# Hymba and PEER layer: the second norm by token half, two projection groups and six query groups re-split, and a last stage of four blocks by token half

## The chip, the cores and the metric
The kernel runs on one core of one Trainium2 chip. Its engines are TensorE (PE in the profile, its weight loads PEld), VectorE (DVE), ScalarE (ACT), GpSimd (POOL) and SyncE (SP), which here only issues the loads. Each runs its own list of instructions in order and waits for the others at semaphores. The metric is the time of one execution on the device in microseconds.

## What is computed
One layer on a sequence of 256 tokens and 1024 channels, float32. The reference, cut to the parts that the change touches:

```python
mod = silu(c) @ w_ada + b_ada
sh1, sc1, g1, sh2, sc2, g2 = split(mod, 6)
h = rmsnorm(x, norm1_g) * (1 + sc1) + sh1
proj = h @ w_in                      # q, k, v of 4 differential heads and 8 block heads
mix = concat(diff_attention, block_attention) @ w_out
x = x + g1 * mix
h2 = rmsnorm(x, norm2_g) * (1 + sc2) + sh2
q = h2 @ peer_wq                     # 8 heads x 2 keys of 128
s1, s2 = q[:, :, 0] . keys1, q[:, :, 1] . keys2     # 128 scores a list, 16 lists
# top 16 of each list, top 16 of their 256 sums: 16 experts a head
x = x + g2 * sum(softmax(score) * gelu(h2 . u[expert]) * v[expert])
out = rmsnorm(x, final_g)
```

## The kernel before
Tokens are two halves of 128 (index t), channels eight chunks of 128 (index c). A number is split where full precision is wanted with fast products: a rounded copy (high, made by ScalarE) and what is left (low, a subtraction on VectorE or GpSimd); a product of two such numbers is three products, high by high, low by high, high by low. A product of unsplit float32 is one instruction of the program and two records of the trace.

Weights come in groups of 256 columns (GROUPS): 0 to 11 for w_in, 12 to 15 for w_out (WO), 16 to 23 for the queries (WQ).

Start: the row c is loaded to all 128 partitions (crow) and put through Silu by ScalarE. VectorE forms the columns of sh1 and sc1 as sums over crow, two per chunk (L1104), ScalarE normalises x together with VectorE (nat), TensorE turns it to columns (L688), ScalarE scales it (hT). Each chunk then meets the weights of groups 0 to 5 (whole_chunk), the first chunks plain (L764, L768), later ones split (L795 to L805).

Attention: 16 units a (8 differential, 8 block ones). For each TensorE makes the scores (L850), VectorE adds the bias (logits, L1216), ScalarE takes the exponential (exps), VectorE weighs the two maps of a differential unit (combine), TensorE transposes (L869) and weighs v (L885). Between the units TensorE works off the projection groups 6 to 11 in quarters (STEPS, proj_step), four a unit, all plain. Into the gaps of VectorE the function sums(a, n) puts the columns of sc2 (units 3 to 6), the row of g1 (7 to 10) and the first columns of sh2. After unit LATE + 1 it multiplies the differential heads by their norm.

Then come the four groups of the output projection (out_highs, out_lows), the residual by group (residual), the sums of squares, the second norm of both token halves at once and the transposes (L688). The eight query groups follow (query_high, query_lows, query_group), with the high copies by ScalarE (high_group) and the low parts by VectorE for group 0 and by GpSimd for 1 to 7 (L430); beside them VectorE adds up the row of g2 (gate_sum, L1091 and L1094). Then 32 score products (L966).

The longest part streams 256 blocks of expert weights, 128 of u and 128 of v: a load into one of five slots, high (L605), low (GpSimd L439 or VectorE L1367), products. While blocks 0 to 46 of u run, VectorE sorts; blocks in SORT_LOW have their low part made by VectorE in the middle of the sort, the others below POOL_LOW = 46 by GpSimd, all later ones by VectorE. The last LAST blocks of v are done by token half, so that the last norm of half 0 runs beside half 1.

SyncE issues all loads in program order, on one queue, with the waits that free their places.

## Time and profile before
| | us |
|---|---|
| median of 3 runs | 980.34 (980.28 to 980.77) |
| the profiled execution | 980.4 |
| its span, first to last instruction | 978.5 |
| TensorE busy in it | 947.8 (97%) |
| VectorE, ScalarE, GpSimd busy | 718.8, 468.2, 161.8 |
| first product of the projection | 15.16 |
| first product of the output projection | 127.6 |
| first score product | 209.1 |
| first product with v blocks | about 622 |

Times in the rows are microseconds from the start of the span. A row of a timeline gives start, duration, engine, line, what is written and read, how many, and in brackets how long the engine was idle before it and what released it. "issue" is time for which the profile shows no wait. The line numbers are those of the kernel before.

### The profile page before, as it was taken

The numbers are of one execution on the slowest core, as the hardware profiler recorded it, in microseconds if no ns is written. First come the engines' busy times: TensorE is split into PE (matmuls) and PEld (weight loads), VectorE is DVE, ScalarE is ACT, GpSimd is POOL, SyncE is SP. The second block draws the span as 40 slices with busy tenths as digits, with TensorE's granted clock in tenths as the row PEclk, the third lists the DMA queues.
The fourth block names the chain that finished last, engine by engine and source line by source line (L and its number), as shares of the span: only waits on it lengthen the run. The fifth ranks groups of instructions, "written<-read, shape, count | busy, mean of one in ns | idle before, by whom it ended". The sixth has DMA issues, their size and how long they took to land.

```text
span 978.5 us, 16499 instructions
## 1 busy us (share of the span) xinstructions
PE 947.8 (97%) x6426; PEld 864.5 (88%) x6426; DVE 718.8 (73%) x1388; ACT 468.2 (48%) x856; POOL 161.8 (17%) x83
## 2 busy tenths in 40 slices
PE   4999998999999999999999999999999999999996
PEld 3987798999999999999999999888888888888885
DVE  4738888729999888999999995655555555555556
ACT  3443665444444534444444444455555555555554
POOL 1000003959889810000000000000000000000000
PEclk9999998999999999999999999999999999999999
DMA  8999457026665555554455555666666666666663
GB/s 341 357 399 436 194 238 317 28 109 184 184 182 185 179 166 159 161 157 152 152 156 166 153 152 176 185 195 191 194 193 195 192 196 191 193 195 194 192 194 115
DMA packets 47900, 193.14 MB, mean 197 GB/s; under 512 B 5312, under 2 KB 7504, under 8 KB 46544
## 3 DMA queue, kind: packets, MB, share of 16 engines
q1 hardware_dynamic: 47760, 192.07, 59.6%
q8 instruction: 51, 0.84, 0.4%
q14 instruction: 25, 0.20, 0.1%
q0 software_dynamic: 64, 0.03, 0.0%
HBM read 191.00 MB, written 1.07 MB: 196 GB/s over the span
## 4 chain that ended last, share of the span: by engine, by line
PE 89%; DVE 4%; POOL 3%; ACT 1%; DMA 1%; issue 1%; SPq 0%; DVEq 0%; ACTq 0%
PE banks L1010 23%; PE banks L986 12%; PE banks L990 12%; PE banks L1017 12%; PE banks L987 12%; PE banks L768 4%; PE banks L1001 3%; POOL wq_low L430 3%; PE banks L764 2%; PE banks L734 2%; PE banks L700 1%; PE banks L802 1%; DMA small_cols<-in_cols 1%; PE banks L751 1%; PE banks L885 1%
## 5 line engine op out<-in xcount | busy, mean ns | idle before, releaser
L1367 DVE TENSOR_TENSOR lo<-raw,hi 128x1024 fp32r<-128x1024 f32 x214 | 267.6, 1251 | 170.5 <-ACT hi L605 169.2
L605 ACT ACTIVATE hi<-raw 128x1024 fp32r<-128x1024 f32 x256 | 271.5, 1061 | 169.7 <-PE banks L1017 169.7
L986 PE MATMUL banks<-h2r,hi 128*128 128x256 f32 x1024 | 256.4, 288 | 0.0
L987 PE MATMUL banks<-h2r,hi 128*128 128x256 f32 x1024 | 251.1, 283 | 0.0
L1010 PE MATMUL banks<-hi,wsplit 128*128 128x512 f32 x1000 | 247.0, 389 | 0.5 <-DVE wsplit L1460 0.5
L1010 PEld LDWEIGHTS banks<-hi,wsplit 128*128 128x128 f32 x1000 | 187.6, 188 | 39.6 <-issue 0.7
L987 PEld LDWEIGHTS banks<-h2r,hi 128*128 128x128 f32 x1024 | 196.5, 192 | 0.0
L986 PEld LDWEIGHTS banks<-h2r,hi 128*128 128x128 f32 x1024 | 196.0, 191 | 0.0
L990 PE MATMUL banks<-h2r,lo 128*128 128x256 f32 x1024 | 143.7, 283 | 2.2 <-DVE lo L1367 2.0
L990 PEld LDWEIGHTS banks<-h2r,lo 128*128 128x128 f32 x1024 | 132.1, 192 | 2.6 <-DVE lo L1367 2.2
L1017 PE MATMUL banks<-lo,wsplit 128*128 128x512 f32 x500 | 133.6, 389 | 0.0
L439 POOL TENSOR_TENSOR lo<-raw,hi 128x1024 fp32r<-128x1024 f32 x42 | 115.6, 2767 | 26.0 <-ACT hi L605 25.7
L1017 PEld LDWEIGHTS banks<-lo,wsplit 128*128 128x128 f32 x500 | 93.8, 188 | 19.5
L624 ACT ACTIVATE gelu_out<-banks 128x256 f32<-128x256 f32 (+32 forms) x74 | 21.7, 293 | 130.3 <-PE banks L990 130.3
L626 ACT ACTIVATE act<-banks 128x256 f32<-128x256 f32 (+32 forms) x117 | 37.8, 323 | 83.9 <-PE banks L990 83.9
L430 POOL TENSOR_TENSOR wq_low<-wq,high 128x1024 fp32r<-128x1024 f32 x14 | 41.7, 3020 | 154.5 <-DVE wq_low L1312 154.5
L1460 DVE TENSOR_TENSOR wsplit<-act,wsplit 128x256 fp32r<-128x256 f32 x128 | 53.4, 417 | 0.4 <-ACT wsplit L645 0.4
L645 ACT ACTIVATE wsplit<-act 128x256 fp32r<-128x256 f32 x128 | 51.2, 400 | 0.0
L1436 DVE TENSOR_TENSOR oh2g<-oh,part_h 128x512 f16<-128x512 f16 x128 | 48.2, 417 | 0.0
L1001 PE MATMUL banks<-oh2g,oh 128*128 128x128 f16 x512 | 40.6, 220 | 0.0
L700 PE MATMUL banks<-h2r,high 128*128 128x256 f32 x256 | 33.3, 290 | 0.0
L700 PEld LDWEIGHTS banks<-h2r,high 128*128 128x128 f32 x256 | 32.2, 197 | 0.6 <-issue 0.5
(207 smaller groups left out, 943.0 us busy)
## 6 DMA issues: line engine op xcount, KB each, us to landing
raw<-in_u_t SPq DMA_DIRECT2D x128, 512.0 KB, 3.6
raw<-in_v_b SPq DMA_DIRECT2D x128, 512.0 KB, 3.6
g_w<-in_w_gate SPq DMA_DIRECT2D x2, 4096.0 KB, 17.0
wq<-in_wq SPq DMA_DIRECT2D x2, 4096.0 KB, 21.3
sh_w<-in_w_mod SPq DMA_DIRECT2D x8, 512.0 KB, 13.6
sc_w<-in_w_mod SPq DMA_DIRECT2D x8, 512.0 KB, 14.2
win<-in_w_in SPq DMA_DIRECT2D x8, 512.0 KB, 14.6
win<-in_w_in SPq DMA_DIRECT2D x1, 4096.0 KB, 21.0
```

The costliest lines, as they stand in the source:

```text
L430: nc.gpsimd.tensor_tensor(low_of[name][:, :, c], full[name][:, :, c], high_slot(w)[:, :, e * P:(e + 1) * P].bitcast(F32), ALU.subtract).th ...
L439: nc.gpsimd.tensor_tensor(lo_t[n % RAW][:, :], raw[n % RAW][:, :], hi_t[:, n % HI, :].bitcast(F32), ALU.subtract).then_inc(pool_low, 1)
L605: nc.scalar.activation(hi_t[:, n % HI, :], raw[n % RAW][:, :], ACT.Copy).then_inc(high_ready, 1)
L700: nc.tensor.matmul(out, high[:, c, e * P:(e + 1) * P], h2r[:, part, c, :], start=(first and c == 0 and part == 0), stop=False, skip_group_ ...
L986: nc.tensor.matmul(dst, w, h2r[:, 0, c, :], start=(c == 0), stop=False)
L987: nc.tensor.matmul(dst, w, h2r[:, 1, c, :], start=False, stop=False)
L990: last = nc.tensor.matmul(dst, lo_t[n % RAW][:, c * P:(c + 1) * P], h2r[:, 0, c, :], start=False, stop=(c == DC - 1))
L1001: last = nc.tensor.matmul(bank[g_bank(g)][:, k * KEYS:(k + 1) * KEYS], oh1[:, g % 2, k // PT, :, k % PT], oh2g[:, g % 2, e, k // PT, :, k ...
L1010: nc.tensor.matmul(bank[2 * t + half][:, :], wsplit[:, j % WS, e, t * P:(t + 1) * P], hi_t[:, n % HI, half * 512:half * 512 + 512], start= ...
L1017: last = nc.tensor.matmul(bank[2 * t + half][:, :], wsplit[:, j % WS, 0, t * P:(t + 1) * P], lo_t[n % RAW][:, half * 512:half * 512 + 512] ...
L1367: nc.vector.tensor_tensor(lo_t[n % RAW][:, :], raw[n % RAW][:, :], hi_t[:, n % HI, :].bitcast(F32), ALU.subtract).then_inc(vector_low, 1)
L1460: nc.vector.tensor_tensor(wsplit[:, j % WS, 1, :], act[:, j, :], wsplit[:, j % WS, 0, :].bitcast(F32), ALU.subtract).then_inc(wl_ready, 1)
```

## The change
It edits seven places.

1. The row c is loaded once (c_line, 4 KB), put through Silu, and spread to 128 partitions by two TensorE products with a row of ones; ScalarE and VectorE copy one half each. small_cols is loaded ahead of the first weights, lam behind the last. The first norm is scaled in column halves, all by ScalarE. Groups 0 to 2's chunks get hh copies too.
2. Projection groups 7 and 8 (HALVED) are computed in three rounded products (halved_step) instead of plain. ScalarE makes their high parts (step_part), VectorE their low parts (step_rest). g1 is loaded in two halves, after group 8.
3. The multiply by the differential heads' norm moves one unit later (LATE + 2).
4. The last output group runs by token half (out_by_rows). VectorE adds and squares each half by itself (last_residual), each half has its own root, and the transposes go by half (rows_to_columns). The squares of the other three groups are two operations of 768 columns. The last column of sh2 moves behind the transposes.
5. Query groups 2 to 7 (the third to the eighth) write high by both halves of h2 as one product of 512 columns (query_wide); ScalarE copies the right half of the two banks (corr), VectorE adds the left half to it (query_sum). VectorE makes the low parts of groups 0 and 1, GpSimd those of 2 to 7. The row of g2 is spread after group 6.
6. SORT_LOW names block 42 in place of 43.
7. LAST is 4, the last block has places of its own (high_at, split_at). At the end VectorE multiplies half 1 by final_g before the root is there, and VectorE and ScalarE scale one column half each.

```diff
+HALVED = (7, 8)
 SPLIT = {"win0": 3, "win1a": 6}
 LATE = 11
-LAST = 3
+LAST = 4
 EXP_AT = 38
 POOL_LOW = 46
-SORT_LOW = (15, 19, 24, 43)
...
+SORT_LOW = (15, 19, 24, 42)
...
-sp.dma_start(crow[:, :], c_row.broadcast_to([P, D])).then_inc(crow_in, 16)
+sp.dma_start(c_line[:, :], c_row).then_inc(crow_in, 16)
...
+sp.dma_start(small_cols[:, :], cols).then_inc(small_in, 16)
 load_mod(0)
-sp.dma_start(small_cols[:, :], cols).then_inc(small_in, 16)
...
-load("g1", g1_w, w_gate[0])
+sp.wait_ge(group_done, HALVED[-1] + 1)
+for n in range(2):
+    load("g1" + "ab"[n], g1_w[n], w_gate[0][:, n * DC // 2:(n + 1) * DC // 2, :])
...
-pool.wait_ge(query_low, 1)
-for w, (name, col) in list(enumerate(GROUPS))[WQ + 1:]:
+pool.wait_ge(query_low, 4)
+for w, (name, col) in list(enumerate(GROUPS))[WQ + 2:]:
...
-nc.scalar.activation(crow[:, :], crow[:, :], ACT.Silu).then_inc(crow_ready, 1)
+nc.scalar.activation(c_line[:, :], c_line[:, :], ACT.Silu).then_inc(line_ready, 1)
...
+sc.wait_ge(line_spread, 1)
+nc.scalar.activation(crow[:, 0:512], bank[0], ACT.Copy).then_inc(crow_ready, 1)
...
-nc.scalar.activation(nat[:, 0, :], xs[:, 0, :], ACT.Copy, scale=rstd[:, 0, 0:1]).then_inc(xn_ready, 1)
+for half in range(2):
+    cols = slice(half * 512, (half + 1) * 512)
+    for t in range(TT):
+        last = nc.scalar.activation(nat[:, t, cols], xs[:, t, cols], ACT.Copy, scale=rstd[:, 0, t:t + 1])
+    last.then_inc(xn_ready, 1)
...
+def step_part(n):
+    name, col = GROUPS[HALVED[n]]
+    sc.wait_ge(loaded[name], 16)
+    sc.wait_ge(group_done, WHOLE)
+    nc.scalar.activation(step_high[n][:, :, :], full[name][:, :, col:col + GW], ACT.Copy
+                         ).then_inc(step_ready, 1)
...
 exps(0)
+step_part(0)
 for a in range(UNITS):
+    if a == 1:
+        step_part(1)
     if a + 1 < UNITS:
...
+high_group(WQ)
+high_group(WQ + 1)
+sc.wait_ge(x1_ready, N_OUT - 1)
+for t in range(TT):
+    nc.scalar.activation(nat[:, t, 0:D - GW], xs[:, t, 0:D - GW], ACT.Square, scale=D ** -0.5,
+                         accum_out=sq_cols[:, t, 0:1]).then_inc(squared, 1)
...
-nc.scalar.activation(rstd[:, 1, :], sq[:, 1, :], ACT.Sqrt).then_inc(rooted, 1)
+nc.scalar.activation(rstd[:, 1, 0:1], sq[:, 1, 0:1], ACT.Sqrt, bias=eps_col).then_inc(rooted, 1)
 sc.wait_ge(rstd_ready, 2)
-sc.wait_ge(squared, 1 + TT * N_OUT)
-nc.scalar.activation(nat[:, 1, :], xs[:, 1, :], ACT.Copy, scale=rstd[:, 1, 1:2]).then_inc(xn_ready, 1)
+sc.wait_ge(squared, 1 + TT)
+nc.scalar.activation(nat[:, 0, :], xs[:, 0, :], ACT.Copy, scale=rstd[:, 1, 0:1]).then_inc(xn_ready, 1)
+sc.wait_ge(var_ready, 4)
+nc.scalar.activation(rstd[:, 1, 1:2], sq[:, 1, 1:2], ACT.Sqrt, bias=eps_col).then_inc(rooted, 1)
+sc.wait_ge(rstd_ready, 3)
+nc.scalar.activation(nat[:, 1, D // 2:D], xs[:, 1, D // 2:D], ACT.Copy, scale=rstd[:, 1, 1:2]
+                     ).then_inc(second_right, 1)
...
+    if g < 2:
+        nc.scalar.activation(qT[:, 2 * g:2 * g + 2, :].rearrange("p a s -> p (a s)"), bank[4 + g],
+                             ACT.Copy).then_inc(q_out, 1)
+    else:
+        b = query_banks(g)
+        if g >= 4:
+            sc.wait_ge(q_sum, g - 3)
+        nc.scalar.activation(corr[:, g % 2, :, :], banks[:, b:b + 2, SEQ:2 * SEQ], ACT.Copy
+                             ).then_inc(q_corr, 1)
...
+        both = bank[query_banks(g) + e].rearrange("p (k s) -> p k s", k=2)
+        for c in range(DC):
+            nc.tensor.matmul(both, high[:, c, e * P:(e + 1) * P], h2r[:, :, c, :], start=(c == 0), stop=False,
+                             skip_group_check=True)
+    for e in range(2):
+        pe.wait_ge(group_low, 2 * (g - 2) + 1 + e)
+        for c in range(DC):
+            last = nc.tensor.matmul(bank[query_banks(g) + e][:, 0:SEQ],
+                                    low_of[name][:, c, col + e * P:col + (e + 1) * P], h2r[:, 0, c, :],
+                                    start=False, stop=(c == DC - 1), skip_group_check=True)
+    last.then_inc(group_done, 1)
...
+def out_by_rows(g):
+    pe.wait_ge(group_high, g + 1)
...
+        out_high(g, e, range(DC))
+        out_low_half(g, e).then_inc(group_done if e else first_rows_done, 1)
...
+def halved_step(g, e, quarter):
+    n = HALVED.index(g)
+    name, col = GROUPS[g]
+    out, part_of = bank[3][:, e * 256:(e + 1) * 256], slice(e * P, (e + 1) * P)
+    high, low = step_high[n], low_of[name]
+    tokens = GIVES[g][0] == "v"
+    if (e, quarter) == (0, 0):
+        pe.wait_ge(step_ready, n + 1)
+        pe.wait_ge(proj_out, g)
+        pe.wait_ge(hh_high, DC)
+        pe.wait_ge(hh_low, DC)
+    chunks = range(2 * quarter, 2 * quarter + 2)
+    for c in chunks:
+        for part in range(2):
+            if tokens:
+                nc.tensor.matmul(out, hh[:, part, c, part_of], high[:, c, :],
+                                 start=(e == 0 and c == 0 and part == 0), stop=False, skip_group_check=True)
+            else:
+                nc.tensor.matmul(out, high[:, c, part_of], hh[:, part, c, :],
+                                 start=(e == 0 and c == 0 and part == 0), stop=False, skip_group_check=True)
+    if quarter == 0:
+        pe.wait_ge(step_low, 2 * n + (2 if tokens else e + 1))
+    for c in chunks:
+        if tokens:
+            last = nc.tensor.matmul(out, hh[:, 0, c, part_of], low[:, c, col:col + GW],
+                                    start=False, stop=(c == DC - 1), skip_group_check=True)
+        else:
+            last = nc.tensor.matmul(out, low[:, c, col + e * P:col + (e + 1) * P], hh[:, 0, c, :],
+                                    start=False, stop=(c == DC - 1), skip_group_check=True)
+    if (e, quarter) == (1, 3):
+        last.then_inc(group_done, 1)
...
+pe.wait_ge(line_ready, 1)
+for half in range(2):
+    nc.tensor.matmul(bank[half], ones[0:1, :], c_line[0:1, half * 512:half * 512 + 512], start=True, stop=True
+                     ).then_inc(line_spread, 1)
...
-for g in (2, 3):
-    out_highs(g)
-    out_lows(g)
+out_highs(2)
+out_lows(2)
+out_by_rows(3)
...
-pe.wait_ge(xn_ready, TT + TT)
-to_columns(nat, x2T_ready, range(DC), place_h2)
+pe.wait_ge(xn_ready, TT + 1)
+rows_to_columns(0, range(DC - 1))
+pe.wait_ge(x1_ready, N_OUT + 1)
+rows_to_columns(0, range(DC - 1, DC))
+pe.wait_ge(second_left, 1)
+rows_to_columns(1, range(DC // 2))
+pe.wait_ge(second_right, 1)
+rows_to_columns(1, range(DC // 2, DC))
...
-    pe.wait_ge(h2_split, b + 1)
-    for g in range(2):
-        for e in range(2):
-            query_high(WQ + g, bank[4 + g], e, range(2 * b, 2 * b + 2), e == 0)
+    for part in range(2):
+        pe.wait_ge(h2_split if part else h2_high, b + 1)
+        for g in range(2):
+            for e in range(2):
+                query_high(WQ + g, bank[4 + g], e, range(2 * b, 2 * b + 2), e == 0, (part,))
...
-    if g >= 4:
-        pe.wait_ge(q_out, g - 3)
-    query_group(WQ + g, bank[4 + g % 4])
-    if g == 5:
+    if g == 4:
+        pe.wait_ge(q_out, 2)
+    if g >= 5:
+        pe.wait_ge(q_sum, g - 4)
+    query_wide(WQ + g, g)
+    if g == 6:
...
+def step_rest(n):
+    name, col = GROUPS[HALVED[n]]
+    ve.wait_ge(step_ready, n + 1)
+    for e in range(2):
+        cols = slice(col + e * P, col + (e + 1) * P)
+        nc.vector.tensor_tensor(low_of[name][:, :, cols], full[name][:, :, cols],
+                                step_high[n][:, :, e * P:(e + 1) * P].bitcast(F32), ALU.subtract
+                                ).then_inc(step_low, 1)
...
+    if a in (0, 2):
+        step_rest(a // 2)
...
+    if a == LATE + 2:
         for t in range(TT):
...
+def last_residual(t):
+    cols = slice(D - GW, D)
+    if t == 0:
+        ve.wait_ge(first_rows_done, 1)
+    else:
+        ve.wait_ge(group_done, N_IN + N_OUT)
+    src = bank[7][:, 0:GW] if t == 0 else bank[3][:, 0:GW]
+    link(nc.vector.tensor_tensor(nat[:, t, cols], src, g1b[:, cols], ALU.mult))
+    nc.vector.tensor_tensor(xs[:, t, cols], xs[:, t, cols], nat[:, t, cols], ALU.add).then_inc(x1_ready, 1)
+    ve.wait_ge(x1_ready, N_OUT + t)
+    ve.wait_ge(squared, 1 + TT)
+    nc.vector.tensor_tensor_reduce(out=nat[:, t, cols], in0=xs[:, t, cols], in1=xs[:, t, cols],
+                                   scale=1.0 / D, scalar=sq_cols[:, t, 0:1], op0=ALU.mult, op1=ALU.add,
+                                   accum_out=sq[:, 1, t:t + 1]).then_inc(var_ready, 1)
+last_residual(0)
+mod2("sh2", sh2_w, 1, range(6, 7), sh2_read)
+ve.wait_ge(rooted, 3)
+nc.vector.reciprocal(rstd[:, 1, 0:1], rstd[:, 1, 0:1]).then_inc(rstd_ready, 1)
 ve.wait_ge(sc2_read, DC)
 ve.wait_ge(sh2_read, DC - 1)
 modulate(a2, 1, slice(0, DC))
-residual(3)
-ve.wait_ge(x1_ready, N_OUT)
-nc.vector.tensor_tensor_reduce(out=nat[:, 0, D - GW:D], in0=xs[:, 0, D - GW:D], in1=xs[:, 0, D - GW:D],
-                               scale=1.0, scalar=0.0, op0=ALU.mult, op1=ALU.add,
-                               accum_out=sq_cols[:, 0, N_OUT - 1:N_OUT]).then_inc(squared, 1)
-ve.wait_ge(squared, 1 + TT * N_OUT)
-link(nc.vector.tensor_reduce(sq[:, 1, :], sq_cols[:, :, :], AX.X, ALU.add))
-nc.vector.tensor_scalar(sq[:, 1, :], sq[:, 1, :], 1.0 / D, EPS, ALU.mult, ALU.add).then_inc(var_ready, 1)
-ve.wait_ge(rooted, 3)
-nc.vector.reciprocal(rstd[:, 1, :], rstd[:, 1, :]).then_inc(rstd_ready, 1)
-ve.wait_ge(rstd_ready, 2)
-nc.vector.tensor_scalar(nat[:, 0, :], xs[:, 0, :], rstd[:, 1, 0:1], None, ALU.mult).then_inc(xn_ready, 1)
-mod2("sh2", sh2_w, 1, range(DC - 1, DC), sh2_read)
-ve.wait_ge(sh2_read, DC)
+last_residual(1)
+ve.wait_ge(rooted, 4)
+nc.vector.reciprocal(rstd[:, 1, 1:2], rstd[:, 1, 1:2]).then_inc(rstd_ready, 1)
+ve.wait_ge(rstd_ready, 3)
+nc.vector.tensor_scalar(nat[:, 1, 0:D // 2], xs[:, 1, 0:D // 2], rstd[:, 1, 1:2], None, ALU.mult
+                        ).then_inc(second_left, 1)
...
-for e in range(2):
-    low_part(WQ, (e, e + 1), query_low)
-gate_sum(acc_g2, "g2", g2_w, range(DC))
+for w in (WQ, WQ + 1):
+    for e in range(2):
+        low_part(w, (e, e + 1), query_low)
+def query_sum(g):
+    b = query_banks(g)
+    ve.wait_ge(q_corr, g - 1)
+    nc.vector.tensor_tensor(qT[:, 2 * g:2 * g + 2, :], banks[:, b:b + 2, 0:SEQ], corr[:, g % 2, :, :],
+                            ALU.add).then_inc(q_sum, 1)
+for c in range(DC):
+    gate_sum(acc_g2, "g2", g2_w, range(c, c + 1))
+    if c in (3, 5, 7):
+        query_sum(2 + (c - 3) // 2)
+query_sum(5)
+query_sum(6)
...
-for half in range(2):
-    end_scale(1, halves2[half])
+ve.wait_ge(squared, 1 + TT + 2)
+nc.vector.tensor_scalar(sq[:, 2, 1:2], sq_cols[:, 1, 0:1], EPS, None, ALU.add).then_inc(var_ready, 1)
+end_residual(1, halves2[1], 3)
+ve.wait_ge(x2_ready, 3)
+nc.vector.tensor_tensor(peer[:, 1, :], xs[:, 1, :], final_gb[:, :], ALU.mult).then_inc(weighed, 1)
+ve.wait_ge(rooted, 6)
+nc.vector.reciprocal(rstd[:, 2, 1:2], rstd[:, 2, 1:2]).then_inc(rstd_ready, 1)
+ve.wait_ge(rstd_ready, 4)
+ve.wait_ge(weighed, 1)
+ve.wait_ge(squared, 1 + TT + 3)
+nc.vector.tensor_scalar(xs[:, 1, 0:D // 2], peer[:, 1, 0:D // 2], rstd[:, 2, 1:2], None, ALU.mult
+                        ).then_inc(final_ready, 1)
```

VectorE's list at units 0 to 2 of the attention, before; logit is the biased score, rsum to prob are combine, sc_w is a column of sc2:

```order
L1216 TENSOR_TENSOR logit<-banks,bias 128x512
L1219 TENSOR_REDUCE nmax<-logit 128x2
L1227 RECIPROCAL rsum<-psum__154 128x2
L1228 TENSOR_SCALAR rlam<-rsum,neglam 128x1
L1229 TENSOR_SCALAR prob<-prob,rlam 128x256
L1231 SCALAR_TENSOR_TENSOR prob<-prob,rsum 128x256
L1216 TENSOR_TENSOR logit<-banks,bias 128x2x128
L1219 TENSOR_REDUCE nmax<-logit 128x2
```

The same place after the change, units 2 and 3:

```order
L1374 TENSOR_TENSOR logit<-banks,bias 128x512
L1377 TENSOR_REDUCE nmax<-logit 128x2
L1385 RECIPROCAL rsum<-psum__163 128x2
L1386 TENSOR_SCALAR rlam<-rsum,neglam 128x1
L1387 TENSOR_SCALAR prob<-prob,rlam 128x256
L1389 SCALAR_TENSOR_TENSOR prob<-prob,rsum 128x256
L1348 TENSOR_TENSOR win_low<-win_61,step_high_77 128x8x128 x2
L1374 TENSOR_TENSOR logit<-banks,bias 128x2x128
```

The two subtractions for group 8 stand between combine(2) and logits(4); two more, for group 7, stand in the same way behind combine(0).

ScalarE's list there, before (prob is exps, qk and probT are copies from banks):

```order
L504 ACTIVATE prob,psum__154<-logit,nmax 128x128 x4
L494 ACTIVATE qk<-banks 128x512
L514 ACTIVATE probT<-banks 128x128
L504 ACTIVATE prob,psum__154<-logit,nmax 128x256 x2
L514 ACTIVATE probT<-banks 128x128
```

And after:

```order
L541 ACTIVATE prob,psum__163<-logit,nmax 128x128 x2
L532 ACTIVATE step_high_76<-win1b 128x2048
L541 ACTIVATE prob,psum__163<-logit,nmax 128x128 x2
L523 ACTIVATE qk<-banks 128x512
L551 ACTIVATE probT<-banks 128x128
L532 ACTIVATE step_high_77<-win_61 128x2048
L541 ACTIVATE prob,psum__163<-logit,nmax 128x256 x2
```

The copy of win2 (win_61) now stands ahead of the exponentials of unit 2.

VectorE's list from the last column of sh2 to the queries, before (acc_g is the row of g2, h2r the split h2):

```order
L1143 TENSOR_TENSOR h2r<-hT,h2r 128x512 x2
L1312 TENSOR_TENSOR wq_low<-wq_62,high_74 128x8x128 x2
L1091 TENSOR_SCALAR acc_g_114<-g_w,cact 128x1024
L1094 SCALAR_TENSOR_TENSOR acc_g_114<-g_w,cact,acc_g_114 128x1024 x7
L1361 TENSOR_TENSOR g2b<-banks,g2b 128x1024
```

And after:

```order
L1287 TENSOR_TENSOR h2r<-hT,h2r 128x512 x2
L1473 TENSOR_TENSOR wq_low<-wq_63,high_79 128x8x128 x2
L1473 TENSOR_TENSOR wq_low<-wq_63,high_80 128x8x128 x2
L1230 TENSOR_SCALAR acc_g_123<-g_w,cact 128x1024
L1233 SCALAR_TENSOR_TENSOR acc_g_123<-g_w,cact,acc_g_123 128x1024 x3
L1540 TENSOR_TENSOR qT<-banks,corr 128x512
L1233 SCALAR_TENSOR_TENSOR acc_g_123<-g_w,cact,acc_g_123 128x1024 x2
L1540 TENSOR_TENSOR qT<-banks,corr 128x512
L1233 SCALAR_TENSOR_TENSOR acc_g_123<-g_w,cact,acc_g_123 128x1024 x2
L1540 TENSOR_TENSOR qT<-banks,corr 128x512 x3
L1551 TENSOR_TENSOR g2b<-banks,g2b 128x1024
```

Two low parts came over from GpSimd, and the sums of the queries lie between those of the row.

## Rows read from the trace of the kernel before
**Rows 1.** The page, part 1: busy time, share of the span, instructions.
```profile
PE 947.8 (97%) x6426; PEld 864.5 (88%) x6426; DVE 718.8 (73%) x1388; ACT 468.2 (48%) x856; POOL 161.8 (17%) x83
```
**Rows 2.** Stretches: from:to, length, busy time (count) by engine, clock, DMA share, GB/s.
```profile
80.00:100.00 20.00, 19.93 (x104) 16.01 (x104) 18.52 (x40) 6.98 (x26) 0.00 (x0) 1.00 1.01 430
...
140.00:160.00 20.00, 15.84 (x114) 15.58 (x113) 17.00 (x31) 11.14 (x23) 0.00 (x0) 0.84 0.34 132
```
**Rows 3.** Timeline of the start.
```profile
15.16 3.78 PE L768 MATMUL banks<-hT,win 128*128 128x256 f32 x8 [1.07 <-ACT hT L527]
```
**Rows 4.** DMA issues to 130 us: what, queue, count, KB each, us to landing.
```profile
win<-in_w_in SPq DMA_DIRECT2D x1, 4096.0 KB, 21.0
...
crow<-in_c_row SPq DMA_DIRECT2D x1, 512.0 KB, 4.1
```
**Rows 5.** Chain that ended last: start, us, what.
```profile
28.90 1.73 PE banks L768 x8
...
35.81 0.24 PE banks L802 x2
...
625.18 1.81 PE banks L1010 x8
```
**Rows 6.** Timeline of VectorE in the attention.
```profile
57.99 0.43 DVE L1216 TENSOR_TENSOR logit<-banks,bias 128x256 f32<-128x256 f32 x1 [6.17 <-DMA bias<-bias_table]
...
74.86 0.42 DVE L1216 TENSOR_TENSOR logit<-banks,bias 128x256 f32<-128x256 f32 x1 [1.87 <-PE banks L850]
...
84.22 0.69 DVE L1216 TENSOR_TENSOR logit<-banks,bias 128x512 f32<-128x512 f32 x1 [0.52 <-PE banks L850]
```
**Rows 7.** Timeline at the end of the attention.
```profile
120.89 0.68 DVE L1216 TENSOR_TENSOR logit<-banks,bias 128x512 f32<-128x512 f32 x1
...
125.62 1.91 ACT L466 ACTIVATE high<-wo 128x2048 fp32r<-128x2048 f32 x1
```
**Rows 8.** Timeline of the second norm.
```profile
150.91 0.69 DVE L1319 TENSOR_TENSOR nat<-banks,g1b 128x512 f32<-128x512 f32 x1 [1.46 <-PE banks L751]
...
153.74 1.15 ACT L588 ACTIVATE nat<-xs,rstd 128x1024 f32<-128x1024 f32 x1 [0.23 <-DVE rstd L1346]
...
155.03 3.65 PE L688 MATMUL banks<-ident,nat 128*128 128x128 f32 x16 [4.16 <-ACT nat L588]
...
158.40 3.83 PE L700 MATMUL banks<-h2r,high 128*128 128x256 f32 x22
```
**Rows 9.** Stretches of one microsecond there, columns as in rows 2.
```profile
154.00:155.00 1.00, 0.00 (x0) 0.00 (x0) 1.00 (x2) 0.89 (x1) 0.00 (x0) 0.50 0.00 0
...
161.00:162.00 1.00, 1.00 (x11) 1.00 (x10) 1.00 (x2) 1.00 (x1) 0.00 (x0) 1.00 1.21 524
```
**Rows 10.** Instructions of wq_low: engine, count, ns min/median/max, first and last start.
```profile
L430 POOL TENSOR_TENSOR wq_low<-wq,high x14: 2385/3334/3395, 162.8 to 202.2; 128x1024 fp32r<-128x1024 f32 x14
L1312 DVE TENSOR_TENSOR wq_low<-wq,high x2: 1216/1216/1217, 161.5 to 162.7; 128x1024 fp32r<-128x1024 f32 x2
```
**Rows 11.** Timeline of the queries, two places.
```profile
182.37 1.21 PE L713 MATMUL banks<-h2r,wq_low 128*128 128x256 f32 x8 [0.66 <-POOL wq_low L430]
...
197.85 1.23 DVE L1361 TENSOR_TENSOR g2b<-banks,g2b 128x1024 f32<-128x1024 f32 x1 [7.77 <-PE banks L693]
```
**Rows 12.** Timeline at the end of the sort.
```profile
336.42 3.06 DVE L1367 TENSOR_TENSOR lo<-raw,hi 128x1024 fp32r<-128x1024 f32 x1 [2.69 <-ACT hi L605]
...
353.23 1.22 PE L990 MATMUL banks<-h2r,lo 128*128 128x256 f32 x8 [1.97 <-DVE lo L1367]
```
**Rows 13.** Instructions of lo, 255 to 360 us, columns as in rows 10.
```profile
L439 POOL TENSOR_TENSOR lo<-raw,hi x27: 2393/2411/4568, 258.2 to 342.2; 128x1024 fp32r<-128x1024 f32 x27
```
**Rows 14.** Timeline of the end.
```profile
965.47 0.70 PE L1044 MATMUL banks<-hi,wsplit 128*128 128x512 f32 x2 [0.28 <-DVE wsplit L1460]
...
971.20 0.69 DVE L1501 TENSOR_TENSOR peer<-banks,g2b 128x512 f32<-128x512 f32 x1
...
975.32 0.99 SPq L400 DMA_DIRECT2D out<-xs  x2
```

216 lines of the change are left out of this document (122 added, 94 removed).

## The prediction
> **What bounds the kernel now.** I read the page first. It shows TensorE busy for 947.8 us of a span of 978.5 [rows 1], so a faster engine elsewhere is worth only what TensorE waits for it, and the change has to be priced at TensorE's gaps and at the work taken from it. The two long stages at the end (256 weight blocks, from 216 us on) are nearly without gaps, and the change adds and removes no product in them. The gaps lie in the first 215 us and around the sort. The table of stretches shows the two kinds: between 80 and 100 us TensorE (19.93 of 20) and VectorE (18.52) are both nearly full, and between 140 and 160 TensorE works 15.84 of 20 at a granted clock of 0.84 [rows 2]. Then I went through the timelines of these places. The profiled execution took 980.4 us (span 978.5 and 1.9 around it), the median is 980.34, so a saving found in this trace comes off the median as it is.
>
> **Start (to the first product).** The first product starts at 15.16 us, released by ScalarE's hT, which waited for VectorE's first column sums [rows 3]. The loads are one queue at about 0.4 MB a microsecond; the row c, copied to 128 partitions, is its first 512 KB and lands after 4.1 us [rows 4]. The change loads 4 KB and spreads the row by two TensorE products, one copy each on ScalarE and VectorE; small_cols goes ahead of the weights. What stands behind comes 0.5 MB / 0.4 = 1.3 us earlier, and with lam (0.13 MB) moved to the end 1.6 us earlier from the third chunk on. The new chain (load 4.5, Silu 5.6, two slow products 9.2, copies 9.9) ends where the reciprocal is due anyway, 10.0 us. I take 1.6 us for the first product, between 0 (if the two products are slower than I take them) and 2.7 (all that chunk 6's load, which has 1.1 us to spare before its products, would let through). The three extra hh copies on ScalarE and three subtractions on VectorE lie in the 6.17 us in which VectorE waits for the bias table [rows 6], so they cost nothing.
>
> **Groups 7 and 8 in three products.** A plain projection quarter is two fp32 products, 4 records and 0.86 us: eight records take 1.73 [rows 5]. A rounded one takes 0.12 us, two are 0.24 [rows 5]. A group is 16 x 0.432 = 6.92 us plain and 48 x 0.12 = 5.76 halved, so TensorE's work falls by 2 x 1.16 = 2.3 us. New on ScalarE are two copies of 128x2048 (1.91 each, as [rows 7]), new on VectorE four subtractions of 1.22 us (as wq_low, [rows 10]), 4.9 us. The second copy stands ahead of exps(2) in ScalarE's queue and waits for win2, 4 MB that take 21.0 us to land [rows 4], from 46.7 to 67.7; behind it stand exps(2), then VectorE's combine(2), the new subtractions and logits(4). With the loads 1.6 us earlier ScalarE is through it at 68.1, exps(2) at 69.1, combine(2) at 70.9, the subtractions at 73.4. TensorE wants them at 72.9: a stall of half a microsecond. The larger effect comes next: logits(4) started at 74.86 and the next wait of VectorE is 0.52 us at 84.22 [rows 6]; it is the tight engine until the last combine. So logits(4) at 73.4 (-1.5), and the 0.5 of that wait gone: **2.0 us** stay at about 98 us, not 1.6 + 2.3 = 3.9. Bounds: 0.5 (win2 lands as before) and 3.9.
> g1 now waits for group 8 and is loaded in halves. Issued at about 80.6, they land by 88 and 93, and are wanted at 92.5 and 102.6. That costs nothing.
>
> **The moved multiply.** It stood ahead of logits(14) and now follows it. logits(15) starts at 120.89 and waits for nothing but VectorE [rows 7]. logits(14) itself cannot start before its scores (118.8), so the multiply ends at 121.3 and logits(15) comes 0.4 later. The chain of the last unit and ScalarE's high copy of wo behind it (125.62, [rows 7]) move with it: **+0.4 us**, bounds -0.8 (what unit 14's exps gain) and +1.3 (the whole multiply).
>
> **Second norm by token half.** Now the last group's sums reach VectorE at 150.91, the scaling copies start at 153.74 and take 1.15 us, the transposes start at 155.03 after a gap of 4.16 and the first query product at 158.40 [rows 8]. After: group 3 finishes its first token half 24 x 0.12 = 2.9 us earlier, at 148.0. Residual and squares (256 columns, half of [rows 8]'s 0.69 each, and 0.5) end at 149.6, the root at 149.8; the reciprocal stands behind one sh2 chunk (1.28) and ends at 151.0, the copy at 152.1. The second half starts at 150.9, ends at 152.6, root, reciprocal and two half copies at 153.7. The first transposed chunk is there at 153.8, and the first query product, which now waits only for the high half, starts at 155.0: 3.4 us earlier.
> The clock: TensorE stopped at 150.9, the granted clock was 0.50 at 154 to 155, its lower level of 1.2 GHz, and back at 1.00 at 161 [rows 9]. After the change the same stretch has gaps of 1.3, 0.6 and 1.2 us with transposes between. If the clock falls all the same, the slower transposes move VectorE's chain by 0.65 us; what it costs the products is hidden by the next paragraph. The Trainium skill, "TensorE: Matmul & The Clock Gate", Part 1, says that the low level is the default and activity lifts it, which would leave the full clock through these shorter gaps; by it the sum is 0.3 lower than with my mean.
>
> **Queries.** A 512-column product takes 0.227 us (eight in 1.81, [rows 5]) against two of 0.12: 16 x 0.013 = 0.2 us a group, 1.3 for six. They don't count, because GpSimd is late. It makes 14 halves of wq_low, 2.385 us each alone and 3.334 at the median, while VectorE's eight gate sums run beside it [rows 10]. TensorE waits for it even now: 0.66 us at 182.37 [rows 11]. After: VectorE makes four halves itself, from 160.0 to 165.0, and GpSimd starts its 12 at 165.0 instead of 162.8. The first eight run beside the gate sums, 26.7 us, and end at 191.7; with them group 5 can end. What follows is TensorE's: 0.96 + (3.63 + 1.92) + 1.72 (mod row) + (3.63 + 1.92) = 13.8, so 205.5 us instead of 209.26: -3.75. With the slow clock, -3.1. I take **-3.4** for norm and queries together. Bounds: -7.6 (GpSimd never waited for) and 0.
> The six new sums on VectorE read a bank and one tile. The one such operation beside a busy GpSimd, g2b, took 1.23 us for 1024 columns [rows 11], no longer than when alone; so 0.7 us each, in time that VectorE spends waiting for GpSimd, and none is needed by TensorE within 6 us. The Trainium skill, "SBUF — State Buffer", section "SBUF: two separate sides", says the pair of ports is locked for a whole instruction by a VectorE operation with two SBUF inputs, so that the other fully blocks. By it eight pairs would take 8 x (2.385 + 1.28) = 29.3 rather than 26.7 and the sum would be 2.6 higher; the trace's 3.334 decides.
>
> **Sort.** VectorE waits 2.69 us for the high part of block 43 at 336.42, and then everything to block 46 is VectorE's, for which TensorE waits 1.97 at 353.23 [rows 12]. With block 42, whose high part is there, the wait falls out: VectorE is 2.7 earlier, and TensorE's wait is gone: **-2.0**. Late next is nothing within 0.7 us. Bounds: -2.2 and 0, the latter if GpSimd's step beside VectorE takes 4.57 as the longest did [rows 13].
>
> **End.** TensorE's last wait, 0.28 (0.44 by its cadence) at 965.47 [rows 14], becomes two of 0.25 and 0.28: +0.1. Token half 0 is finished 1.36 us earlier against the end, and the last quarter's path from 971.20 to the store at 975.32 (4.1 us, [rows 14]) loses a 0.15 us step and part of the scaling, but an extra multiply of 1.2 us stands before it; worked out 3.8, and the second store follows 0.5 behind. **-0.4**, bounds -1 and +0.5.
>
> **Sum.** -2.0 + 0.4 - 3.4 - 2.0 - 0.4 = -7.4; 980.4 - 7.4 = **973.0 us**.
>
> **Rivals.**
> A, less is left: win2 lands as late as before and VectorE keeps 0.5 instead of 2.0, the clock falls: 980.4 - 0.5 + 0.4 - 3.1 - 2.0 - 0.4 = 974.8, or 976 if half the sort's gain goes too. For it speaks that every step added before 100 us is on the two engines that are not idle there. Chance 0.24.
> B, more is left: VectorE and ScalarE follow TensorE to 100 us (-1.9), the clock stays up and the gate sums overlap GpSimd less (-1.5): 969.6. Against it stands the missing wait in VectorE's rows between 75 and 84 us. Chance 0.14.
> C, slower: the new sums on VectorE lock GpSimd out, and its step takes 4.57, its longest in this trace [rows 13]. Twelve end at 165.0 + 54.8 = 219.8, queries at 220.8, 11.5 later than now: 980.4 - 2.0 + 0.4 + 11.5 - 2.0 - 0.4 = 987.9. It decides from 4.1 us a step on. The g2b row speaks against it. Chance 0.03.
> D, the change doesn't do what it says: the two extra waits per group (subtraction, sum) eat both halved groups and wide products, and the norm's halves end together; then the sort and a little of the start are left, 978 to 979. Chance 0.03.
> The forecast has 0.56.
>
> **Numbers.** The range is 969.5 to 976.0: it takes in the forecast and nearly all of A and B. About 0.2% (2 us) is what a measurement tells from no change: faster 0.95, same 0.02, slower 0.03.
>
> **What would show it.** First product at 13.5. logits(4) at about 73.4, and TensorE waiting for VectorE's combine at 75 to 77. The transposes of the norm between 152 and 156, first query product near 155 of a trace that is 1.6 us ahead, so 153.4; GpSimd's 12 steps without a gap and TensorE waiting for them in groups 3 to 5. No wait for block 46. The sum is wrong if GpSimd's steps are not 3.3 us, or if VectorE is not the tight engine between 75 and 98 us.

## The result, and the profile after

Four runs of the changed kernel have a median of **969.36 us** (968.73 to 969.73), the kernel before 980.53 (980.28 to 980.77) beside it: a ratio of 0.9882, interval 0.9868 to 0.9897. The change takes 11.2 us; 7.4 were forecast, and the median lies 0.14 us below the stated range. The profiled execution took 968.99, its span 967.1.

The page, part 1, of after (before in [rows 1]): TensorE is 1.4 us less busy and the span 11.4 shorter, so for 10 of the 11.4 us TensorE had stood still before.
```profile
PE 946.4 (98%) x6366; PEld 857.4 (89%) x6366; DVE 728.9 (75%) x1406; ACT 475.7 (49%) x858; POOL 158.7 (16%) x81
```
Where the time went, by landmarks read from both traces (us from the start of each span):

| landmark | before | after | moved, and the stage's share |
|---|---|---|---|
| first product of the projection | 15.16 | 12.39 | -2.77 |
| logits(0), released by the bias table | 57.99 | 54.80 | -3.19 |
| logits(4) | 74.86 | 71.32 | -3.54 |
| logits(13) | 115.99 | 111.71 | -4.28 |
| first product of the output projection | 127.59 | 123.69 | -3.90: attention **-3.90**, forecast -1.6 |
| last product of it ends | 150.88 | 146.98 | -3.90 |
| first query product | 158.40 | 151.49 | -6.91: norm -3.01 (-2.6 against e3 and e13, see e10) |
| first score product | 209.10 | 200.41 | -8.69: queries -1.78; both **-4.79**, forecast -3.4 |
| first u block | 216.16 | 207.48 | -8.68 |
| u block to TensorE's last product | 755.00 | 753.03 | sort **-1.97**, forecast -2.0 |
| last product to the span's end | 7.34 | 6.59 | **-0.75**, forecast -0.4 |

Two stages give more than was worked out for them: the attention 2.3 us, the norm with the queries 1.4.

TensorE's timeline of after at the start (row: start, us, engine, line, what; in brackets the wait and what ended it), against [rows 3]:
```profile
3.38 3.75 PE L947 MATMUL banks<-c_line,ones 1*128 1x512 f32 x4 [3.38 <-ACT c_line L473]
10.14 1.94 PE L744 MATMUL banks<-ident,nat 128*128 128x128 f32 x8 [3.02 <-ACT nat L488]
12.39 3.78 PE L847 MATMUL banks<-hT,win 128*128 128x256 f32 x8 [0.31 <-ACT hT L564]
...
17.04 1.03 PE L847 MATMUL banks<-hT,win 128*128 128x256 f32 x4
```
The same engine in before: the thirteenth record of the projection, and the first wait after 15.16, which is at 117.78. Between the two TensorE has no wait that the profile shows.
```profile
20.44 1.11 PE L768 MATMUL banks<-hT,win 128*128 128x256 f32 x4
...
117.78 0.41 PE L869 MATMUL banks<-ident,prob 128*128 128x128 f32 x2 [0.29 <-ACT probT L514]
```
In the attention of after, first VectorE (against [rows 6]), then ScalarE at the landing of win2 (the 4 MB with the weights of group 8), then TensorE:
```profile
54.80 0.42 DVE L1374 TENSOR_TENSOR logit<-banks,bias 128x256 f32<-128x256 f32 x1 [5.12 <-DMA bias<-bias_table]
```
```profile
64.88 1.91 ACT L532 ACTIVATE step_high<-win 128x2048 fp32r<-128x2048 f32 x1 [2.48 <-DMA win<-in_w_in]
```
```profile
71.46 0.50 PE L879 MATMUL banks<-win_low,hh 128*128 128x256 f32 x2 [0.46 <-DVE win_low L1348]
...
74.69 0.44 PE L989 MATMUL banks<-ident,prob 128*128 128x128 f32 x2 [0.57 <-DVE prob L1389]
```
The second norm in after (before: [rows 8] and [rows 9]), TensorE's timeline and two stretches of 1 us: the one gap of 4.16 is three gaps, and the granted clock, 0.50 before, stays at 1.00.
```profile
148.16 1.06 PE L1060 MATMUL banks<-ident,nat 128*128 128x128 f32 x8 [1.19 <-ACT nat L623]
149.53 1.09 PE L1060 MATMUL banks<-ident,nat 128*128 128x128 f32 x8 [0.30 <-DVE nat L1523]
151.49 0.71 PE L756 MATMUL banks<-h2r,high 128*128 128x256 f32 x4 [0.87 <-ACT h2r L508]
```
```profile
150.00:151.00 1.00, 0.62 (x6) 0.39 (x4) 0.92 (x2) 0.81 (x2) 0.00 (x0) 1.00 0.61 262
151.00:152.00 1.00, 0.51 (x4) 0.54 (x5) 0.69 (x3) 0.97 (x3) 0.00 (x0) 1.00 0.91 393
```
The queries in after (before: [rows 10] and [rows 11]): the chain that ended last goes through eight steps of GpSimd, 3.16 us each; then TensorE's two waits for GpSimd, and VectorE's wait for ScalarE's corr.
```profile
161.06 25.25 POOL wq_low L453 x8
```
```profile
173.97 1.22 PE L785 MATMUL banks<-h2r,wq_low 128*128 128x256 f32 x8 [0.56 <-POOL wq_low L453]
...
186.35 1.22 PE L785 MATMUL banks<-h2r,wq_low 128*128 128x256 f32 x8 [0.84 <-POOL wq_low L453]
```
```profile
173.63 0.69 DVE L1540 TENSOR_TENSOR qT<-banks,corr 128x512 f32<-128x512 f32 x1 [1.97 <-ACT corr L642]
```
The end of after, VectorE's last scaling and the last store (before: [rows 14]): 960.51, the end of the last product, to 963.95 is 3.44 us; before it was 971.16 to 975.32, 4.16.
```profile
963.43 0.49 DVE L1717 TENSOR_SCALAR xs<-peer,rstd 128x512 f32<-128x512 f32 x1
```
```profile
963.95 0.82 SPq L423 DMA_DIRECT2D out<-xs  x2
```

### The profile page after: what moved, and what is told of

Its sections match the earlier page's. It is cut to its first block, busy times and chain, and to the rows that moved or that the text cites. A ratio compares the mean times of both kernels' runs of the same rounds, so it can differ in the third digit from the quotient of the medians.

```text
span 967.1 us, 16417 instructions
## 1 busy us (share of the span) xinstructions
PE 946.4 (98%) x6366; PEld 857.4 (89%) x6366; DVE 728.9 (75%) x1406; ACT 475.7 (49%) x858; POOL 158.7 (16%) x81
## 4 chain that ended last, share of the span: by engine, by line
PE 89%; DVE 5%; POOL 3%; ACT 1%; issue 1%; DMA 1%; SPq 0%; DVEq 0%; ACTq 0%
PE banks L1149 23%; PE banks L1125 13%; PE banks L1129 12%; PE banks L1126 12%; PE banks L1156 12%; PE banks L1140 3%; PE banks L847 3%; POOL wq_low L453 3%; PE banks L843 2%; PE banks L800 1%; DVE sc_w L1264 1%; PE banks L916 1%; PE banks L780 1%; PE banks L1105 1%; PE banks L816 1%
## 5 line engine op out<-in xcount | busy, mean ns | idle before, releaser
L462 POOL TENSOR_TENSOR lo<-raw,hi 128x1024 fp32r<-128x1024 f32 x42 | 118.6, 2839 | 24.3 <-ACT hi L656 24.0
L453 POOL TENSOR_TENSOR wq_low<-wq,high 128x1024 fp32r<-128x1024 f32 x12 | 35.6, 3009 | 154.0 <-DVE wq_low L1473 154.0
L1638 DVE TENSOR_TENSOR act<-banks,act 128x216 f32<-128x216 f32 (+31 forms) x64 | 32.5, 508 | 0.3 <-issue 0.3
L1140 PEld LDWEIGHTS banks<-oh2g,oh 128*128 128x128 f16 x512 | 29.4, 97 | 2.8
```

The source lines that it names most:

```text
L453: nc.gpsimd.tensor_tensor(low_of[name][:, :, c], full[name][:, :, c], high_slot(w)[:, :, e * P:(e + 1) * P].bitcast(F32), ALU.subtract).th ...
L462: nc.gpsimd.tensor_tensor(lo_t[n % RAW][:, :], raw[n % RAW][:, :], hi_t[:, n % HI, :].bitcast(F32), ALU.subtract).then_inc(pool_low, 1)
L1140: last = nc.tensor.matmul(bank[g_bank(g)][:, k * KEYS:(k + 1) * KEYS], oh1[:, g % 2, k // PT, :, k % PT], oh2g[:, g % 2, e, k // PT, :, k ...
```

## Experiments

"Out" is the first product of the output projection and "score" the first score product, in us of the run's own span; medians stand beside the kernel before on the same chip. The same kernel's way from the bias table to out varies between traces by 0.4 us (68.89 in the trace above, 68.47 in another one of it). Other marks are steadier. From logits(4) to out it is 52.34 to 52.38 in twelve traces of the changed kernel and its variants. From the landing of win2 to logits(4) it is 6.46 or 6.47 in nine of them.

### The start: what brought the 3.5 us at logits(4)

**e1, the row c loaded 128-fold again.**
```diff
-sp.dma_start(c_line[:, :], c_row)
+sp.dma_start(crow[:, :], c_row.broadcast_to([P, D]))
```


> The changed kernel, but the row c is again loaded to 128 partitions (512 KB, first in the queue), put through Silu by ScalarE as a whole, and not spread by TensorE; small_cols keeps its early place. Theory L (the 128-fold copy of the row held the load queue for about 2.4 us, not for the 1.3 us that 0.5 MB at 0.4 MB/us gave): first product at about 15 instead of 12.39, first product of the output projection at about 126.9 instead of 123.69, time 969.4 + 3.2 = 972.6. Theory of the prediction (1.3 us for the row, the rest from the order of the loads): first product at 13.7, time 970.9.

970.25 against 981.03 (0.9895). First product 14.19 (+1.80), but the bias table 55.52 (+0.72) and out 124.25 (+0.56). The 512 KB cost the first product more than the 1.3 us that they take in the queue, and the attention a third of that delay: both expectations were off. The third isn't a clean price: in this trace the slow pace behind the first product (see e3) was short, 3.67 us for the first twelve records against 4.65 in after, which gives TensorE 1.0 back.

**e2, small_cols loaded behind the weights again.**
```diff
-sp.dma_start(small_cols[:, :], cols)
 load_mod(0)
+sp.dma_start(small_cols[:, :], cols)
```


> The changed kernel, but small_cols is loaded behind the first chunk of sh1 and sc1 again, as before. Theory L: its place is worth at most 0.3 us, time 969.4 to 969.7. Rival O (the chain of before runs through small_cols, issued at 3.66 and waited for until 11.7, so its place sets the first column sums): they start when it lands, about 1 us later, first product at 13.4, time 970.4.

970.27 against 981.03 (0.989). First product 12.99 (+0.60), out 123.85 (+0.16). In before this load was on the chain to the first product (chain of before, then the DMA issues of before and of after: KB and us to landing):
```profile
3.66 8.06 DMA small_cols<-in_cols
```
```profile
small_cols<-in_cols SPq DMA_DIRECT2D x1, 24.5 KB, 8.1
```
```profile
small_cols<-in_cols SPq DMA_DIRECT2D x1, 24.5 KB, 4.2
```
It explains 0.6 of the first product's 2.77, and e1 another 1.80. This trace also lost 2 us in the sort; see there.

**e3, the kernel before with eight products of ones at the start**, to ask whether an earlier clock is what the two spreading products bring.
```diff
+for n in range(8):
+    nc.tensor.matmul(bank[0][:, 0:P], ones[:, :], ones[:, :], start=True, stop=True)
```


> The kernel before, with eight products of ones by ones (128 columns, float32) on TensorE as soon as the row c has landed, from about 4.9 to 8.7 us; their result is overwritten, the output is unchanged. Theory C (part of the changed kernel's gain at the start is TensorE's clock: its first products at 3.38 us bring the half-rate stretch to an end sooner): the first product stays at 15.16, but the product rate doubles at about 16 to 17 instead of 20.2, 0.7 to 0.9 us less, time 979.5. Rival: the products change nothing, 980.4.

980.60 against 981.03 (0.9996, interval 0.9986 to 1.0005): no difference can be told in the time. The trace shows more. Two stretches of e3 around its start (columns as in [rows 2]):
```profile
18.00:19.00 1.00, 1.00 (x4) 0.82 (x3) 0.13 (x1) 0.42 (x1) 0.00 (x0) 0.50 1.02 329
20.00:21.00 1.00, 1.00 (x6) 0.87 (x6) 0.85 (x1) 0.00 (x0) 0.00 (x0) 1.00 1.05 426
```
Eight records take 3.78 us while the granted clock is 0.50 and 1.73 later. The first twelve took 4.61 us here and 5.28 in before, 0.67 less. The first split products came 0.7 us earlier (34.76 for 35.46), logits(4) 0.70 (74.16), out 0.23, the first u block 0.69. Then the stall in the sort was followed by the lower clock, which cost 1.5 (see the sort). So a sooner full rate does reach logits(4) in the kernel before. Whether the products of ones brought it is open: the twelve take 5.3 in e10, whose start is that of before, but 4.1 in e13, which has no such products. When the full rate sets in differs from trace to trace, in the changed kernel and its variants too (3.39 to 5.28 us for the twelve).

**e9, lam loaded early again, all else changed.**
```diff
+sp.dma_start(lam_in[:, :], lam.broadcast_to([P, 4 * DH]))
 load_mod(2)
```
(its later load is gone, and its two sums on VectorE are back ahead of the third chunk's)

> The changed kernel, but lam is again loaded ahead of the third chunk, and VectorE again waits for it and forms its two sums between the second and the third chunk's column sums, as before. Theory Q (the part of the start that the prediction missed is this wait, 1.35 us, with 0.65 us of work behind it, in the queue of the engine whose column sums release the load of the bias table): the third chunk's sums start about 1.1 us later, the bias table lands about 1 us later, first product of the output projection at 124.7 instead of 123.69, time 970.4. Rival L (only the bytes ahead in the load queue count, 0.13 MB, 0.3 us): 969.7.

970.91 against 980.85 (0.9894). The bias table releases VectorE at 57.28 (+2.48), out is 125.79 (**+2.10**), twice what theory Q had put down for it. So the changed kernel needs this move. VectorE's timelines show how. Before, it waits for lam with the third chunk's column sums behind:
```profile
19.13 0.22 DVE L1174 CUSTOM_DVE_ANT_0 lam_t<-lam_in 128x64 f32<-128x64 f32 x1 [1.35 <-DMA lam_in<-in_lam]
...
20.42 1.29 DVE L1104 CUSTOM_DVE_ANT_0 sh_w<-sh_w,crow,small_cols 128x1024 f32<-128x1024 f32 x1 [0.91 <-DMA sh_w<-in_w_mod]
```
After:
```profile
18.05 1.28 DVE L1243 CUSTOM_DVE_ANT_0 sh_w<-sh_w,crow,small_cols 128x1024 f32<-128x1024 f32 x1 [1.68 <-DMA sh_w<-in_w_mod]
```
With lam put back (e9):
```profile
18.50 0.23 DVE L1319 CUSTOM_DVE_ANT_0 lam_t<-lam_in 128x64 f32<-128x64 f32 x1 [1.79 <-DMA lam_in<-in_lam]
...
19.79 1.29 DVE L1243 CUSTOM_DVE_ANT_0 sh_w<-sh_w,crow,small_cols 128x1024 f32<-128x1024 f32 x1 [0.92 <-DMA sh_w<-in_w_mod]
...
57.28 0.42 DVE L1374 TENSOR_TENSOR logit<-banks,bias 128x256 f32<-128x256 f32 x1 [6.52 <-DMA bias<-bias_table]
```
The sums release the buffers that the later chunks are loaded into. SyncE's queue goes in order, and the bias table stands behind these loads; it is issued at 45.98 before and at 42.95 after. SyncE issues win1b, the bias table and win2 only when the last column sums are done (42.22 in after), so a delay of the sums delays all three. What the attention feels is win2: it lands at 66.94 in e9 and at 64.86 in after, 2.08 later, and logits(4) and out are 2.09 and 2.10 later. The bias table isn't the mark: in e17, a second trace of the changed kernel, it comes 0.37 later than in after, and win2, logits(4) and out are the same within 0.05. VectorE and ScalarE of e17:
```profile
55.17 0.42 DVE L1374 TENSOR_TENSOR logit<-banks,bias 128x256 f32<-128x256 f32 x1 [5.80 <-DMA bias<-bias_table]
```
```profile
64.85 1.92 ACT L532 ACTIVATE step_high<-win 128x2048 fp32r<-128x2048 f32 x1 [2.70 <-DMA win<-in_w_in]
```
TensorE too waits for the late loads in e9, three times before 50 us (0.83, 0.53 and 0.69), the first for win:
```profile
25.04 0.45 PE L847 MATMUL banks<-hT,win 128*128 128x256 f32 x1 [0.83 <-DMA win<-in_w_in]
```
In after it waits nowhere between 12.39 and 71.46, in before nowhere between 15.16 and 117.78.

**e13, the kernel before with lam alone moved.**
```diff
 load_win(1)
-sp.dma_start(lam_in[:, :], lam.broadcast_to([P, 4 * DH]))
...
+sp.dma_start(lam_in[:, :], lam.broadcast_to([P, 4 * DH]))
 sp.wait_ge(sc1_ready, DC)
```


> The kernel before, with the load of lam behind the last weights of the first stage and VectorE's two sums over it behind its last low part, as in the changed kernel, and nothing else. Theory Q (this move is the largest part of what the start gave: put back into the changed kernel it cost 2.1 us at the output projection): the bias table is there at about 56 instead of 57.99, first product of the output projection at 125.5 instead of 127.59, and GpSimd, the sort and the end keep their waits, time 978.4. Rival: without the row's shorter load VectorE waits for the third chunk all the same, 0.3 us or less, 980.2.

980.84 against 981.40 (0.9995, interval 0.9986 to 1.0004). Both expectations were off, and the time shows no gain. Sums at 19.52 (-0.90), bias table 56.67 (-1.32), logits(4) 73.66 (-1.20), out 126.71 (-0.88), first u block 214.87 (-1.29). From there to TensorE's last product it takes 1.57 more than in before, with the lower clock behind the sort's stall, and the lead is gone. Its VectorE, then TensorE:
```profile
56.67 0.42 DVE L1216 TENSOR_TENSOR logit<-banks,bias 128x256 f32<-128x256 f32 x1 [5.70 <-DMA bias<-bias_table]
```
```profile
15.22 3.41 PE L768 MATMUL banks<-hT,win 128*128 128x256 f32 x8 [1.06 <-ACT hT L527]
...
19.32 1.03 PE L768 MATMUL banks<-hT,win 128*128 128x256 f32 x4
```
It is tempting to read the 0.88 as the worth of lam in the kernel before, but this trace doesn't show that. TensorE waits neither here nor in before between its first product and 116 us, so no load held it up. The lead is there at the thirteenth record (19.32 for 20.44), before the third chunk could matter: the full rate came sooner. In the kernel before and its three variants logits(4) follows the thirteenth record by the same time:

| trace | first product | thirteenth record | logits(4) | between the two |
|---|---|---|---|---|
| before | 15.16 | 20.44 | 74.86 | 54.42 |
| e10 (start unchanged) | 14.75 | 20.04 | 74.46 | 54.42 |
| e3 | 15.22 | 19.83 | 74.16 | 54.33 |
| e13 | 15.22 | 19.32 | 73.66 | 54.34 |
| after | 12.39 | 17.04 | 71.32 | 54.28 |

So before the change the attention is timed by TensorE alone: by its first product and by how soon the full rate comes. The bias table, released at 57.11 in e10 and 58.08 in e3, makes no difference to it. In after this chain and the one from win2 end within 0.3 us of each other. Where the full rate comes soon (e11, e12, e17: 3.4 to 3.7 us for the twelve) win2 decides, and TensorE waits for a part of the weights at 44.5. Where it comes late (e14: 5.28) TensorE decides, with 54.40. The start's part is then 2.77 from the first product and 0.63 from the sooner full rate (4.65 us for the twelve against 5.28), which other traces of either kernel give or take. lam's place alone brings nothing that a run shows; with the first product earlier it keeps the loads from taking 2.1 back.

### The attention

**e4, groups 7 and 8 plain again.**
```diff
-HALVED = (7, 8)
+HALVED = ()
```


> The changed kernel, but groups 7 and 8 are computed in plain float32 as before, without high and low copies. Theory V (VectorE is what attention waits for between 72 and 98 us, so most of TensorE's 2.3 us did not come through): first product of the output projection at 124.1 to 124.5, time 969.8 to 970.2. Rival T (TensorE sets the pace there, and the 2.3 us came through, less the two stalls of 0.46 and 0.57): 1.3 to 2.3 us later, time 970.7 to 971.7.

972.71 against 981.03 (0.9903), where in its trace the sort took 3.6 more (below). Out 124.49, 0.80 later than in after. From logits(4) to out it takes 53.10, and 52.37 in after. So the halved groups bring 0.7 to 0.8 at out, not 2.3, and the place is that of theory V, in which VectorE and ScalarE take the rest. How much they bring ahead of logits(4) this trace can't say, since its full rate came 1.1 us sooner than after's (3.53 us for the first twelve records).

**e14, the multiply one unit earlier again** (with the line of e12 added).
```diff
-if a == LATE + 2:
+if a == LATE + 1:
```


> The changed kernel with the activation of 128x1 that lets VectorE's operation start first in the sort (969.19), and the multiply by the norm of the differential heads where it was, behind unit 12 instead of 13. Theory of the prediction: the moved multiply costs 0.4 us, so 0.4 less, first product of the output projection at 123.3, time 968.8. Rival: VectorE has no room there after the change, 969.2 or more.

969.06 against 981.40 (0.9871). From logits(13) to out it takes 11.61, as in before (11.60); after has 11.98. The moved multiply costs 0.37. Out itself was 124.25, not the 123.3 expected, and the time (968.8 expected) isn't told from e12's 969.19: in this trace the full rate came late (5.28 us for the first twelve records), and logits(4) at 72.26, 0.96 later than in e12.

**e15, half of group 8's low part on GpSimd** (with e12's line).
```diff
+nc.gpsimd.tensor_tensor(low_of[name][:, four, c], full[name][:, four, c],
+                        step_high[1][:, four, :].bitcast(F32), ALU.subtract)
```


> The changed kernel with the same activation, but of group 8's low part VectorE makes the first four chunks and GpSimd, idle there, the last four at the same time; TensorE waits for each only where it needs it. Theory V (TensorE's two stalls of 0.46 and 0.57 at 71 to 75 us are VectorE's two subtractions): both go, 1.0 us less, first product of the output projection at 122.7, time 968.2. Rival P (GpSimd's step and VectorE's next operations with two inputs in SBUF hold each other up): 0.3 us or nothing, 969.0.

968.99 against 981.40 (0.9873). Out is 123.92, not 122.7, and neither theory's 1.0 nor a clear nothing came: from the landing of win2 to logits(4) it takes 6.15, where the same kernel without it takes 6.46 (e12). VectorE is spared 1.22 us and gains 0.31. GpSimd and VectorE of e15:
```profile
67.42 2.41 POOL L451 TENSOR_TENSOR win_low<-win,step_high 128x1024 fp32r<-128x1024 f32 x1 [60.28 <-ACT step_high L537]
```
```profile
68.81 1.18 DVE L1403 TENSOR_SCALAR prob<-prob,rlam 128x256 f32<-128x256 f32 x1
```
After has this operation in 0.35 us at 68.26. Here it ends at 69.99, after GpSimd's step (69.83): an operation with one SBUF input took three times as long beside GpSimd's step, and it takes 1.18 in e16 and e18 too. The Trainium skill, "SBUF — State Buffer", section "SBUF: two separate sides", gives the rule: a VectorE operation in its two-port mode or with two SBUF inputs and a GpSimd operation exclude each other for a whole instruction. The trace agrees, with 1.18 for 0.35, if this operation ran in that mode; no row names the mode.

### The norm and the queries

**e10, the kernel before with 16 products in the norm's gap**, so that the clock stays up.
```diff
+for n in range(16):
+    nc.tensor.matmul(bank[0][:, 0:P], ones[:, :], ones[:, :], start=True, stop=True)
 pe.wait_ge(xn_ready, TT + TT)
```


> The kernel before, with sixteen products of ones by ones (128 columns, float32, about 3.5 us) on TensorE in the gap between the last output product and the transposes of the second norm; their result is overwritten, the output is unchanged. Theory C (the granted clock fell to 0.50 because TensorE stood still for 4.16 us): it stays at 1.00, the transposes take 1.9 instead of 3.65 us, the first 64 query products 7.9 instead of 8.9, and the queries end 1.0 to 1.4 us earlier, time 979.2. Rival G (GpSimd, not TensorE, sets the end of the queries in the kernel before too): only what reaches GpSimd's start comes through, 0.3 to 0.6 us, time 980.0.

982.13 against 980.85 (1.0009, interval 1.0000 to 1.0018); neither expected gain came, and the profiled execution also had the lower clock behind the sort's stall. In the norm the clock did stay at 1.00, and the transposes take 1.91 us for 3.65. TensorE, then GpSimd of e10:
```profile
155.96 1.91 PE L688 MATMUL banks<-ident,nat 128*128 128x128 f32 x16
158.84 7.43 PE L700 MATMUL banks<-h2r,high 128*128 128x256 f32 x60 [0.97 <-DVE h2r L1145]
```
```profile
163.28 41.73 POOL L430 TENSOR_TENSOR wq_low<-wq,high 128x1024 fp32r<-128x1024 f32 x14 [154.98 <-DVE wq_low L1314]
```
The 14 steps take 41.73 as before; from GpSimd's first step to the first score product it is 46.27 against 46.26. The first query product did not even come earlier (158.84 for 158.40; it waited for VectorE). GpSimd alone set the end of the queries before. What the clock was worth this run can't say, because the sixteen products got in the way: they start at 152.28, take 3.84, and the transposes begin at 155.96 where they began at 155.03. A cleaner case is e3, where the stretch at 0.50 was shorter by chance:
```profile
154.81 2.85 PE L688 MATMUL banks<-ident,nat 128*128 128x128 f32 x16 [4.16 <-ACT nat L588]
```
Same gap of 4.16, transposes in 2.85 instead of 3.65. From the last product of the output projection to the first query product it is 7.06 (e13: 7.08) for 7.52 in before, and GpSimd's first step and the score come as much earlier. So the lower clock in the norm did reach GpSimd's start and cost the trace of before some 0.45 us; the norm's 3.01 in the table holds as much of chance.

**e5, the query products 256 columns wide again.**
```diff
-nc.tensor.matmul(both, high[:, c, e * P:(e + 1) * P], h2r[:, :, c, :], ...)
+for part in range(2):
+    nc.tensor.matmul(bank[query_banks(g) + e][:, part * SEQ:(part + 1) * SEQ], ..., h2r[:, part, c, :], ...)
```


> The changed kernel, but the high products of query groups 2 to 7 are again two of 256 columns each, into the same banks; corr, the sums and the split of the low parts stay. Theory G (GpSimd's first eight steps set the end of the queries, as predicted: it is released at 161.06 and its eighth step ends at 186.3 either way): only the groups behind group 5 count, 2 x 0.19 = 0.4 us, time 969.8. Rival T (TensorE is the bound and GpSimd costs it only two short waits): 6 x 0.19 = 1.15, time 970.5.

969.57 against 981.30 (0.9882; after 0.9882). From the first query product to score 49.19, +0.27; the two waits for GpSimd shrink to 0.21 and 0.62. The wide products are TensorE time that it spends waiting, as the prediction had it.

**e6, six of the eight g2 gate sums left out** (the row of g2 that is computed lacks them).
```diff
-gate_sum(acc_g2, "g2", g2_w, range(c, c + 1))
+if c in (0, DC - 1):
+    gate_sum(acc_g2, "g2", g2_w, range(c, c + 1))
```


> The changed kernel, but of the eight sums of the row of g2 six are left out (chunks 1 to 6), so that VectorE works less beside GpSimd. Theory G (a step of GpSimd takes 3.33 beside such a sum and 2.39 alone, and the mean of 3.16 over the first eight is a mixture): the twelve steps take about 12 x 2.4 + 2 x 0.95 = 31 us instead of 35.6, TensorE waits for none of them, 1.4 us less, time 968.0. Rival: the steps are slow for another reason, 35 us, time 969.4.

967.04 against 981.30 (0.9856). From the first query product to score 46.71 (-2.2). Ten of GpSimd's twelve steps now take 2.4 each, and the two beside the gate sums that are left 2.84 and 3.42:
```profile
161.55 9.90 POOL L453 TENSOR_TENSOR wq_low<-wq,high 128x1024 fp32r<-128x1024 f32 x4 [154.37 <-DVE wq_low L1473]
174.01 19.90 POOL L453 TENSOR_TENSOR wq_low<-wq,high 128x1024 fp32r<-128x1024 f32 x8 [2.57 <-ACT high L495]
```
No query product waits for GpSimd any more. VectorE's gate sums beside it are what makes a step 3.3 us, and 2.2 us is all that this is worth: then wq1's load is late (GpSimd waits for ScalarE's high, which waits for it), and TensorE's own work.

**e7, a fifth low part on VectorE**, eleven left for GpSimd.
```diff
-pool.wait_ge(query_low, 4)
+pool.wait_ge(query_low, 5)
+low_part(WQ + 2, (0, 1), query_low)   # VectorE
```


> The changed kernel, but VectorE makes a fifth half of the low parts (the first of group 2) and GpSimd eleven instead of twelve. Theory G: GpSimd starts 1.2 us later and has one step less before each group, 3.2 - 1.2 = 2.0 us earlier at group 5, so both waits of TensorE for it (0.56 and 0.84) go: 1.4 us less, 968.0. Rival: VectorE's later sums (queries, row of g2) become the new wait, which gives 0.5 or more back: 968.5 to 969.5.

968.88 against 981.30 (0.9871). 48.29 from the first query product to score, -0.63. GpSimd, then TensorE of e7:
```profile
173.14 22.81 POOL L455 TENSOR_TENSOR wq_low<-wq,high 128x1024 fp32r<-128x1024 f32 x8 [1.55 <-ACT high L497]
```
```profile
185.61 1.22 PE L790 MATMUL banks<-h2r,wq_low 128*128 128x256 f32 x8 [0.84 <-POOL wq_low L455]
```
The first of the two waits goes, the second stays: GpSimd now waits for wq1 for 1.55 us. The expected 968.0 didn't come. The time lies in the rival's 968.5 to 969.5, with GpSimd's wait for wq1 where the rival had VectorE's sums.

### The sort

**e8, block 43 put back for 42.**
```diff
-SORT_LOW = (15, 19, 24, 42)
+SORT_LOW = (15, 19, 24, 43)
```


> The changed kernel, but SORT_LOW names block 43 as before. If the sort's term holds, VectorE waits some 2.7 us for block 43's high part and TensorE about 2 us for block 46: 971.4. Rival: the earlier start of the stream has moved the loads against the sort so that the wait is gone anyway: 969.4.

971.70 against 981.30 (0.9905). TensorE waits 1.97 at 344.34, and from the u block to the end it is 755.10: the 2.0 of the prediction.

**e11 and e12: who comes first at 320 us.** In e2, e4 and e9 the sort was 2 to 3.6 us longer with block 42. In after VectorE's match started at 320.43 and GpSimd's step, by its clock, at the same time; VectorE went first (2.29), and GpSimd's step took 4.58 (chain). After, VectorE and the chain:
```profile
320.43 2.29 DVE L1601 TENSOR_TENSOR hit<-hit,top_i 128x2048 f32<-128x2048 f32 x1
```
```profile
320.43 4.58 POOL lo L462
```
e11 puts a tiny memset ahead of the match on VectorE, e12 a tiny activation ahead of the block's high part on ScalarE, on which GpSimd's step waits.
```diff
+nc.vector.memset(nmax[:, 0, 0:1], 0.0)                               # e11
```
```diff
+nc.scalar.activation(warm[:, 2:3], ones[:, 0:1], ACT.Exp)            # e12
```


> The changed kernel, with one memset of 128x1 on VectorE between the two operations of 128x2048 at about 320.4 us of the trace of after, so that the second of them starts some 0.1 us behind GpSimd's low part of block 40 instead of in the same 10 ns. Theory P (the two engines want the same port, whoever starts first keeps it for its whole instruction, and the other stands for 2.2 us): VectorE's operation takes 4.5 instead of 2.29 us, everything of the sort behind it is 2.3 us later and TensorE waits about 2 us for block 44, 971.5 in every execution. Rival: the start times are a coincidence, the time is 969.5.

> The changed kernel, with one more activation of 128x1 on ScalarE (0.2 us) behind the exponentials of the gates, so that block 40's high part and with it GpSimd's step come 0.2 us later and VectorE's operation always starts first. Theory P: VectorE's operation takes 2.29 us in every execution, TensorE doesn't wait for block 44, 969.2 with no execution 2 us above the others. Rival: the spread of 969 to 973 seen in other runs of the changed kernel has another source and stays.

e11: 972.19, e12: 969.19, both against 980.85 (0.9908, 0.9881). VectorE, GpSimd and TensorE of e11:
```profile
320.38 4.54 DVE L1603 TENSOR_TENSOR hit<-hit,top_i 128x2048 f32<-128x2048 f32 x1
```
```profile
320.37 2.41 POOL L462 TENSOR_TENSOR lo<-raw,hi 128x1024 fp32r<-128x1024 f32 x1 [2.18 <-ACT hi L656]
```
```profile
344.41 1.49 PE L1129 MATMUL banks<-h2r,lo 128*128 128x256 f32 x8 [1.92 <-DVE lo L1558]
```
Stretches of e11 (columns as in [rows 2]; the clock is the number behind the five engines):
```profile
345.00:346.00 1.00, 1.00 (x8) 1.00 (x7) 0.82 (x2) 0.07 (x1) 0.00 (x0) 0.58 0.00 0
346.00:347.00 1.00, 1.00 (x7) 1.00 (x6) 0.36 (x1) 1.00 (x2) 0.00 (x0) 0.50 0.32 41
347.00:348.00 1.00, 1.00 (x6) 1.00 (x6) 0.95 (x3) 0.26 (x1) 0.00 (x0) 0.50 0.80 180
```
VectorE of e12:
```profile
320.41 2.29 DVE L1602 TENSOR_TENSOR hit<-hit,top_i 128x2048 f32<-128x2048 f32 x1
```
The loser of the pair waits for the winner's whole instruction. When it is VectorE, it is 2.25 us late, TensorE stalls 1.9, and after that stall the clock may fall to its lower level: from the u block to the end it is 753.02 to 753.20 with VectorE first, 755.0 to 755.1 with the stall, 756.4 to 756.6 with stall and lower clock. In both traces of the changed kernel as it is VectorE came first, and all its eight runs lie at the lowest level (968.73 to 969.73), so the three levels expected of e17 did not come and its rival holds. The kernel before hides the tie: there VectorE waits 2.69 us for block 43 anyway, and its stall of TensorE is 1.97 or 2.33 either way (e3, with a match of 4.55). Only the fall of the clock behind that stall shows in it: 755.00 in its own trace, 756.4 to 756.6 in those of e3, e10 and e13.

### The parts that helped, together

**e16**: five low parts on VectorE (e7), the quarter on GpSimd (e15), the multiply early (e14), and e12's line. **e17** is the changed kernel again and **e18** is e16 again, on one chip.

> The changed kernel with the activation in the sort, the quarter of group 8 on GpSimd, the multiply behind unit 12 and the fifth half of the query low parts on VectorE (0.6 us less at the scores by itself). If the parts add up: 969.2 - 1.0 - 0.4 - 0.6 = 967.2. Rival: VectorE's chain to the last unit takes back the first two, 968.5.

> The changed kernel as it is, for how often its executions lose the port race of the sort. Theory P: executions fall on three levels, 969 (VectorE starts first), 971 (GpSimd starts first, TensorE waits 2 us) and 973 (the same, and the granted clock falls in that wait), the lowest the most frequent, median 969.4 to 970. Rival: the first four executions, 968.73 to 969.73, are all there is.

> The kernel of e16 again, beside the changed kernel on the same chip: only the lowest level, since VectorE always starts first, and 1.5 us below the changed kernel's lowest level, 967.7.

e16: 967.71 against 981.40 (0.9864). On the other chip the changed kernel took 969.09 and the new one **967.33**, 1.76 less, against 980.47 for before. In e16's trace out is 122.60 and score 198.64, 1.09 and 1.77 earlier than in after; in e18's they are 0.83 and 1.56 earlier than in e17's. The sum of the parts, 1.0 + 0.4 + 0.6 as expected of e16, put the time at 967.2; 967.71 and 967.33 came.

## Why the prediction was short

**Start and attention: the step that failed.** The prediction took "1.6 us for the first product" and carried it through the loads: "With the loads 1.6 us earlier ScalarE is through it at 68.1", and from there through VectorE, "the tight engine until the last combine", to logits(4) at 73.4 (-1.5). Measured: first product -2.77, win2 landed 2.82 earlier (64.86 for 67.68), logits(4) -3.54 (71.32). Three things were wrong in it.
- The size of the first product's gain. The row's load was worth 1.80 at the first product (e1), where the prediction has 1.3 for it, and the first column sums waited for small_cols (chain of before, e2: 0.6).
- The engine. Before the change TensorE has no wait between 15.16 and 117.78, so VectorE was not what timed the attention there. What comes earlier at TensorE's first product comes earlier at logits(4), as long as the loads keep up. Moving lam is what let them (e9: 2.1), and the prediction priced it by its bytes, 0.3 us, though its wait (1.35 us on VectorE at 19.13) stands ahead of the sums that free the buffers.
- A term put at nothing: TensorE's slow pace behind its first product. [rows 3] has eight records in 3.78 us where [rows 5] has eight in 1.73. In after it ended sooner and gave 0.63, by chance as far as the runs show.

**Groups 7 and 8.** Half right. "2.0 us stay at about 98 us" was one figure for these and the start, and threw the other 1.9 away. The two engines did take most of these groups' gain: e4 gives 0.8 where TensorE's work falls by 2.3. But the start's gain is not in the same account. The prediction's chain from win2 (landing at 66.1 by its 1.6) to logits(4) took 7.3 and measured 6.47. The wait for combine was foreseen at 75 to 77 and came at 74.69 (0.57), with 0.46 at 71.46, the foreseen "stall of half a microsecond". After 75 us TensorE has no wait up to 113.50, so it was TensorE that was tight there. The sum by what the runs show is 2.77 + 0.63 at the thirteenth record, 0.14 more up to logits(4), which no run takes apart, then 0.73 (e4) less 0.37 (e14): 3.90. The last two are differences within the changed kernel; in the kernel before the way from logits(4) to out varies between 52.73 and 53.20, so this part is known to half a microsecond.

**The moved multiply**: +0.4 forecast, +0.37 measured (e14). Right.

**Norm and queries**: -3.4 forecast, -4.79 measured. The norm gave 3.01: the first query product comes 4.51 us after the last product of the output projection, where the prediction has 4.12 (155.0 less 150.88), and the product starts behind 0.87 of waiting for its first high half. The queries were to add nothing to that and added 1.78. The rule "GpSimd sets the end" was right (e10, e5, e6). The sizes, from the first query product on: GpSimd's first step after 9.57, not 10.0 (-0.43); eight steps 25.25, not 26.7 (-1.45); from their end to score 14.10, not 13.8 (+0.30). The failed step is "the first eight run beside the gate sums, 26.7 us". In after VectorE waits 1.97 for corr at 173.63 and does sums from PSUM in between, and one of the eight steps then runs alone; the mean of 3.16 lies between its 3.33 beside the gate sums and its 2.39 alone. With the 0.35 that the forecast held back for a lower clock, the norm's +0.39 and 0.16 by which the landmark of before was read too late, that is the whole: -3.4 - 0.35 + 0.16 - 0.43 - 1.45 + 0.30 + 0.39 = -4.78. The clock stayed at 1.00 in the norm, the better of the two cases that the prediction took the mean of. That TensorE's slower transposes would "move VectorE's chain by 0.65 us" is near what e3 and e13 show against before, 0.45.

**Sort**: -2.0 forecast, -1.97 measured; e8 gives it back. The bound of 0, "if GpSimd's step beside VectorE takes 4.57", had the right mechanism on the wrong engine: it is VectorE's 4.54 that costs (e11). With the lower clock behind the stall it is 1.6 worse than before the change (756.60 in e4 for 755.00), which the bound doesn't cover.

**End**: -0.4 forecast, -0.75 measured, within its bounds; the path from the last product to the store fell by 0.72 where 0.3 was worked out. No run took it apart, so which of its steps was mis-sized stays open. In the traces of e7 and e11 the last store ends 0.9 later after the same steps (7.47 and 7.46 from the last product), so half of such a difference can be the store's.

**Rivals.** B ("more is left") is the nearest, 969.6. That "VectorE and ScalarE follow TensorE to 100 us" is close to what happened, but B took its 1.9 from the halved groups, and what came was from the first product. That the number is so near is in part luck. Its second half, gate sums that overlap GpSimd less, is what the queries show. C (GpSimd locked out by the new sums) did not happen: each PSUM sum took 0.69, and beside these GpSimd got faster. The range ended at B's likeliest time. It had no room for a start worth more than its 1.6, though TensorE has no wait between its first product and 117.78 us in the trace of before.

## What to carry to other kernels

Ask first which engine has no wait in a stage: here it was TensorE, from its first product on, and what came earlier there came through until the loads set the limit. Then price a load by who waits for it and by what stands behind that wait in the waiting engine's queue, not by its bytes: put back into the changed kernel, 128 KB cost 2.1 us, since the sums behind it free the buffers of all later loads. A gain at one landmark in a single trace isn't the worth of the edit: e13's 0.9 was there before the moved load is waited for. When an engine is the one that sets a stage's end, take the duration of its step from the mixture that the new order will give, with the neighbour's waits in it, and leave TensorE's own savings out of the sum. Two instructions that lock each other and start within 10 ns are a coin to be tossed by any edit ahead of them: look for them before comparing variants, and push one of them back.

## What was not expected of the hardware

- A tie between VectorE's match and GpSimd's step is settled by some 10 ns (320.37 against 320.38 us in e11, 320.43 and 320.43 in after), and costs the loser 2.2 us. Edits more than 190 us earlier turned it.
- A stall of TensorE of 1.9 us sometimes brings the lower clock behind it (e11: 0.58, 0.50, 0.50) and 1.5 us more, and sometimes not (e2, e8), in places that look alike.
- A VectorE operation with one SBUF input was held up by GpSimd (e15: 1.18 for 0.35).
- The same first twelve records of the projection took 3.39 to 5.28 us in the traces of nearly the same program, by when TensorE's full rate set in. In the kernel before this came through to logits(4) whole (e3, e13), in the changed one only down to the limit that win2 sets.
- The gap of 4.16 us in the norm was followed by transposes of 3.65 us in before and of 2.85 in e3, which made 0.45 us at the first score product.
